# Clearing the sorted token rows in four parts behind the first weight slots

## The reference

```python
h = rms_norm(x, g_mix);  proj = h @ w_in
mla_out = rms_norm(mla_group(c_q, c_kv, k_rope, ...), g_mla_out)   # 8 heads of latent attention
rw_out = rwkv7_group(feat, ...)                                    # 8 heads of a gated recurrence over 512 steps
x = x + concatenate([mla_out, rw_out], -1) @ w_o
x = x + hier_moe(rms_norm(x, g_ffn), ...)                          # 32 experts, 2 for each token
...
def hier_moe(h, ...):
    for e in range(N_EXPERTS):
        hidden = silu(t @ w_gate[e]) * (t @ w_up[e])
        y = y + combine[:, e:e + 1] * (hidden @ w_down[e])
```

## Time and profile before

| | |
|---|---|
| time, median of three | 2688.33 us |
| the profiled execution's own time | 2689.85 us |
| its span | 2688.0 us |
| TensorE busy | 2414.5 us (90%) |
| VectorE / ScalarE / GpSimd busy | 1057.6 / 745.9 / 650.7 us |
| granted TensorE clock, mean | 0.934 of full |
| the chain that ended last | PE 78%, DMA 7%, DVE 7%, issue 3%, ACT 3% |
| moved by the DMA engines | 301.86 MB |

### The profile page before, as it was taken

How to read it: one execution, slowest core, us unless ns; L and a number is a source line. 1 busy time by engine, 2 the same in 40 slices (tenths; PEclk the granted TensorE clock), 3 DMA queues, 4 the chain that set the end, 5 groups by cost and what they waited for, 6 DMA issues and landing times.

```text
span 2688.0 us, 31483 instructions
## 1 busy us (share of the span) xinstructions
PE 2414.5 (90%) x12390; PEld 1679.0 (62%) x12390; DVE 1057.6 (39%) x1863; ACT 745.9 (28%) x1176; POOL 650.7 (24%) x284
## 2 busy tenths in 40 slices
PE   7989688896777769989999999998988999999998
PEld 2334466544222248657876888887755887688886
DVE  2455455522011151565243656202165423466610
ACT  2333212211111113323222333212343222233311
POOL 0000000001000024213443444443320444344443
PEclk9999788876888879989998999999998999899999
DMA  4101700043999833212322333222210322233322
GB/s 187 47 24 39 144 3 2 2 178 138 406 411 408 327 110 110 64 32 71 96 93 70 95 100 97 79 99 81 91 55 23 95 94 94 70 95 95 101 80 85
DMA packets 80458, 301.86 MB, mean 112 GB/s; under 512 B 6944, under 2 KB 7328, under 8 KB 79808
## 3 DMA queue, kind: packets, MB, share of 16 engines
q1 hardware_dynamic: 72864, 277.97, 30.2%
q10 hardware_dynamic: 5152, 13.58, 1.3%
q0 software_dynamic: 2304, 8.39, 0.9%
HBM read 283.86 MB, written 24.97 MB: 115 GB/s over the span
## 4 chain that ended last, share of the span: by engine, by line
PE 78%; DMA 7%; DVE 7%; issue 3%; ACT 3%; POOL 0%; SPq 0%; DVEq 0%; ACTq 0%; another core or an unknown queue 0%; POOLq 0%
PE bank L1738 12%; PE bank L1740 12%; PE bank L1739 12%; DMA arena<-in_stream 5%; PE bank L527 5%; PE bank L1412 3%; PE bank L1876 3%; PE bank L1878 3%; PE bank L1877 3%; DVE arena L386 2%; PE bank L834 2%; PE bank L1725 2%; DVE arena L392 2%; PE bank L1723 2%; PE bank L1724 2%
## 5 line engine op out<-in xcount | busy, mean ns | idle before, releaser
L1483 POOL TENSOR_TENSOR ring_low<-ring,W_high 128x1024 fp32r<-128x1024 f32 x264 | 635.1, 2406 | 1080.5 <-ACT W_high L396 1080.5
L1738 PE MATMUL bank<-H_high,W_high 128*128 128x512 f32 x1408 | 562.8, 400 | 21.9 <-DVE H_low L386 11.3
L1739 PE MATMUL bank<-H_low,W_high 128*128 128x512 f32 x1408 | 554.5, 394 | 0.0
L1740 PE MATMUL bank<-H_high,ring_low 128*128 128x512 f32 x1408 | 554.1, 394 | 0.0
L396 ACT ACTIVATE W_high<-ring 128x1024 fp32r<-128x1024 f32 x264 | 279.7, 1060 | 974.7 <-PE bank L1740 603.9
L1738 PEld LDWEIGHTS bank<-H_high,W_high 128*128 128x128 f32 x1408 | 267.5, 190 | 102.8 <-issue 27.6
L1740 PEld LDWEIGHTS bank<-H_high,ring_low 128*128 128x128 f32 x1408 | 268.1, 190 | 57.1
L1739 PEld LDWEIGHTS bank<-H_low,W_high 128*128 128x128 f32 x1408 | 268.6, 191 | 55.1 <-issue 1.0
L396 ACT ACTIVATE arena<-bank 128x512 f32<-128x512 f32 (+4 forms) x275 | 130.3, 487 | 466.0 <-PE bank L809 120.2
L392 DVE SCALAR_TENSOR_TENSOR arena<-arena,bank 128x512 f32<-128x512 f32 (+2 forms) x116 | 55.5, 482 | 480.2 <-ACT arena L400 262.3
L1467 POOL DMA_INDIRECT sorted_x<-arena x8 | 7.9, 982 | 638.2 <-DVE arena L386 636.1
(11 more groups left out here) (222 smaller groups left out, 2955.0 us busy)
## 6 DMA issues: line engine op xcount, KB each, us to landing
ring<-in_stream SPq DMA_DIRECT2D x289, 512.0 KB, 3.6
arena<-in_stream SPq DMA_DIRECT2D x32, 2048.0 KB, 13.8
arena<-in_stream SPq DMA_DIRECT2D x32, 1024.0 KB, 10.6
sorted_x<-in_zero_row SPq DMA_DIRECT2D x1, 8704.0 KB, 49.0
arena<-sorted_x SPq DMA_DIRECT2D x17, 512.0 KB, 15.9
sorted_y<-arena ACTq DMA_DIRECT2D x16, 512.0 KB, 7.0
X<-in_x SPq DMA_DIRECT2D x1, 2048.0 KB, 9.0
out<-X ACTq DMA_DIRECT2D x8, 256.0 KB, 2.9
```

Source lines behind the costliest of these rows:

```text
L1483: G.tensor_tensor(ring_low[:, slot, :], ring[:, slot, :], W_high[:, s % 2, :].bitcast(F32), ALU.subtract).then_inc(po.tells("w_split"), 1)
L1738: mm(ps[:, :], wh[:, k, :], H_high[:, k, :], start=k == 0, stop=False)
L1739: mm(ps[:, :], wh[:, k, :], H_low[:, k, :], start=False, stop=False)
L1740: i = mm(ps[:, :], wl[:, k, :], H_high[:, k, :], start=False, stop=k == KD - 1)
```

## The change

The single clearing behind the two spare loads is gone. In its place the slot loop issues four clearings of 544 rows (2.2 MB each), one right behind the load of slots 11, 13, 15 and 17. Each adds 16 to `rows_cleared`, so GpSimd now waits for 64.

```diff
-            e.wait_ge(ev("rows_cleared"), 16)
+            e.wait_ge(ev("rows_cleared"), 4 * 16)
...
+            CLEARED_AFTER, CLEARED_ROWS = (11, 13, 15, 17), (ROWS + P) // 4
             n_in = n_slots["A"] - 8
             for s in range(n_in + R):
                 if s >= R:
...
                 fill(s, "A")
                 if s == 0:
                     e.dma_start(w1, ts_["w1"]).then_inc(ev("w1_in"), 16)
+                if s in CLEARED_AFTER:
+                    part = CLEARED_AFTER.index(s) * CLEARED_ROWS
+                    e.dma_start(sorted_x[part:part + CLEARED_ROWS, :], ts_["zero_row"].to_broadcast([CLEARED_ROWS, D])).then_inc(ev("rows_cleared"), 16)

             sp.e.wait_ge(*sp.nth("mla_out", 4))
             e.wait_ge(slot_full[0], 16 * 4)
             e.dma_start(SPARE_OUT, stream[at0["A"] + 24]).then_inc(slot_full[0], 16)
             e.dma_start(SPARE_HALF, stream[at0["A"] + 25][:, 0:512]).then_inc(ev("half_in"), 16)
-            e.dma_start(sorted_x[0:ROWS + P, :], ts_["zero_row"].to_broadcast([ROWS + P, D])).then_inc(ev("rows_cleared"), 16)
             sp.e.wait_ge(*sp.nth("rw_out", 4))
```

## The result

The changed kernel takes 2673.01 us (median of six runs, 2664.64 to 2673.34) against 2689.14 us for the kernel before in the same session (six runs, 2686.98 to 2691.68): 16.1 us less. The ratio is 0.9934, with a 95% interval of 0.9921 to 0.9947. (Ratios here are the measurement's own, over all fast executions; they differ from the ratio of the two medians by up to 0.0008, which is 2 us.) The forecast was 2673.3 us, range 2667.5 to 2682.0.

A forecast was written before the change was run, and what follows sets the result against it. TensorE's standing still in prepare of c = 0 was taken as the bound. Gains of 5.0 and 12.35 us, less 2.4 for the clock, gave 15 us, counted through to the end: median 2673.3 us, range 2667.5 to 2682.

The forecast's parts named there:

- The mechanism: Prepare of c = 0: TensorE stops three times, 13.70 us, running dry of code whose packets must get past the clearing.
- The rival that the stops have another cause: The stops in prepare of c = 0 aren't code behind the clearing, so nothing changes: 2688 us, chance 0.06.
- The first half of prepare: Prepare of c = 0, up to VectorE taking up the first level: 311.0 instead of 316.01, a gain of 5.0 us.
- code that is late even without the clearing: Prepare of c = 0, line 726: the next code packet may still be late, so 0.6 us is added.
- The three levels: Prepare of c = 0, three levels hit by the stops: 24.56 us becomes 12.2 us, a gain of 12.35 us.
- The clock: Prepare of c = 0: one level's worth at the lower clock, 2.4 us, is taken off the 17.35 us gain.
- the lower bounds: Prepare of c = 0, all of it at the lower clock: the gain would be down to 5 us.
- The first section: Where the four parts are issued behind slots: cost 0 on TensorE, at most one stop of 6.6 us.
- The cover: First section: a code packet lasts some 55 us, so one 11 us late is still early; a factor of four.
- What follows behind: Scan, `w_o`, router, sorting and expert loads after prepare move forward together; the whole 15 us counts to the end.
- The rival that the clock falls elsewhere: Levels of c = 1 to 3 fall to the lower clock, costing 26.5 us against 15: 2700, slower, chance 0.03.
- cutting in four: The clearing split into four parts: makes no single code fetch faster, only the place helps.

## Why the prediction was right

**The mechanism.** TensorE ran out of code behind the clearing. Shown three ways: the stops follow the clearing to c = 2, they vanish on 4 engines at the same place, and they scale with how long a DMA engine takes over the pieces in front. The rival that the stops have another cause (2688) is excluded by this. What was not shown is through which DMA engines the code comes, and how much of the clearing goes ahead of it.

**The first half of prepare.** Forecast 5.0 us from the first masking to the first level. The first masking, before and after:

```profile
303.91 2.08 DVE L386 TENSOR_TENSOR arena<-bank,early 128x256 f32<-128x256 f32 x6 [0.39 <-PE bank L726]
```

```profile
306.31 2.08 DVE L386 TENSOR_TENSOR arena<-bank,early 128x256 f32<-128x256 f32 x6 [0.39 <-PE bank L726]
```

It was 316.01 - 303.91 = 12.10 us and is 312.42 - 306.31 = 6.11 us, 6.0 us less. I had added 0.6 us for code that is late even without the clearing. This term was not needed: the stop there is 0.20 us, and it ends well before TensorE has to wait for VectorE.

```profile
307.84 0.82 PE L726 MATMUL bank<-arena 64*64 64x64 f32 x37 [0.20 <-issue]
310.30 1.15 PE L738 MATMUL bank<-arena 64*64 64x64 f32 x32 [1.64 <-DVE arena L386]
```

**The three levels.** Forecast 12.35 us; 24.56 us became 12.25 (312.42 to 324.67), 12.3 us less.

**The clock.** This term was off. I took away one level's worth, 2.4 us, and the clock was 1.00 throughout. Nor were the lower bounds needed: no kernel with the stops away had its levels at the lower clock. But the term isn't nothing everywhere. With the clearing at c = 2, and on 4 engines, the stretch up to the first level takes 7.4 us and not 6.1. The timeline with the clearing at c = 2:

```profile
303.23 3.01 PE L726 MATMUL bank<-arena 64*64 64x64 f32 x160
307.97 1.67 PE L738 MATMUL bank<-arena 64*64 64x64 f32 x32 [1.73 <-DVE arena L386]
```

No code is late there, since the 160 products go by in one string; lines 738 (1.67 us against 1.15) and 834 run slower, at a granted clock of 0.84 in 303 to 311 (0.83 on 4 engines). In the change it is 1.00. Why the clock differs among these kernels stays open. Without this term the forecast for this stretch would have been 17.4 us, and 18.3 were measured.

**The first section.** Forecast 0, and 0 it is: TensorE is as busy in 60 to 290 us (210.10 us against 210.21). The cover is 55 / 11, which is a factor of five and not the four that the prediction says, and not all of it was used: a packet some 17 us late, in pieces of 1 KB, cost nothing either.

**What follows behind.** Counted through in full, and it was: 2.4 us more came out in the recurrence, 0.5 us in all that follows, and +2.4 us were lost at the start, before the change does anything. These are of the size by which executions of one kernel differ, and the median gained 16.1 us where the two profiled ones differ by 18.8. The rival that the clock falls elsewhere did not come true: from line 764 to the end of the recurrence it is 0.84, against 0.82 before. So the forecast's 15 us comes so near partly because the clock term, wrong by 2.4 us, and such differences lie in opposite directions. That it was met to 0.3 us is luck; that the gain lies between 12 and 18 us is not.

**The part that did no work.** The prediction says that cutting in four makes no fetch faster and that only the place helps. So it is: one piece in the first section and four at the old place settle it.

## What to carry to other kernels

A transfer that nobody waits for is not free: here it filled the DMA engines while TensorE ran through long unrolled code of short instructions, and that code came late. Look for "issue" in the chain while the DMA share is 1.0, and count the instructions between two such stops. Put the transfer beside long instructions (here 4 to 5 instructions a microsecond instead of about 50, and over 100 where the first stop came), or keep it off most of the DMA engines. Making its pieces smaller made it worse.

## What the runs showed that I had not expected

- A clearing from one row of 4 KB moves about 200 GB/s, on 16 engines and on 8 alike, and half of that on 4; a copy from different rows, in packets of 35 KB, moves 320 to 329 GB/s. In pieces of 1 KB it moves 70 GB/s, on 16 engines, on 8 and on 4.
- A packet of code waits behind some 70 to 90 KB of such pieces on its DMA engine, whether they are of 4 KB or of 1 KB (an estimate from a few stops).
